# Splitting the first modulation into two column parts, and turning the order of two MLP steps, in a hybrid attention block

## The reference

```
c_act = silu(c)
mod   = c_act @ w_ada + b_ada            # 1024 -> 6 * 1024
sh1, sc1, gt1, sh2, sc2, gt2 = split(mod, 6)
h = rmsnorm(x, g_norm1) * (1 + sc1) + sh1
proj = h @ w_in          # queries, keys, values of three attention branches, indexer, gates
...                      # indexer scores -> top 128 keys, three attentions, gated merge
x = x + gt1 * (merged @ w_out)
h2 = rmsnorm(x, g_norm2) * (1 + sc2) + sh2
f_g, f_u = split(h2 @ w_gate_up, 2)
x = x + gt2 * ((silu(f_g) * f_u) @ w_down)
out = rmsnorm(x, g_final)
```

## Time and profile before

| | us |
|---|---|
| median of 3 runs | 1027.21 (1025.36 to 1028.98) |
| profiled execution, its time | 1024.62 |
| profiled execution, its span | 1022.8 |
| PE busy | 979.8 (96%) |
| DVE, ACT, POOL busy | 487.1, 382.2, 90.5 |
| first pass of the first projection starts at | 43.97 |
| tile 6 starts at | 80.42 |

### The profile page before, as it was taken

One profiled execution on the slowest core, in us unless ns is written; L12 is line 12 of the kernel. 1 busy time (PEld: TensorE's weight loads), 2 busy tenths in 40 slices (PEclk: granted clock), 3 DMA queues, 4 the chain that ended last, 5 costly groups with the idle time before them and its releaser, 6 DMA issues.

```text
span 1022.8 us, 12488 instructions
## 1 busy us (share of the span) xinstructions
PE 979.8 (96%) x4831; PEld 798.5 (78%) x4831; DVE 487.1 (48%) x826; ACT 382.2 (37%) x677; POOL 90.5 (9%) x130
## 2 busy tenths in 40 slices
PE   2699999999999999999999999999999999999997
PEld 0677988878877777778888888988888888888875
DVE  4845688743335435654647374733343343331323
ACT  4434522345555656642222223432232322221312
POOL 3000000000035432200000002000000000000401
PEclk9799999999999999999999999999999999999999
DMA  8693234321221201164555662123334434232312
GB/s 308 236 294 109 71 99 131 119 83 42 91 99 41 62 22 42 32 205 131 185 193 172 211 225 88 63 83 103 103 109 157 144 104 144 83 103 83 124 41 83
DMA packets 86082, 123.11 MB, mean 120 GB/s; under 512 B 4792, under 2 KB 67861, under 8 KB 85906
## 3 DMA queue, kind: packets, MB, share of 16 engines
q1 hardware_dynamic: 85506, 116.25, 34.8%
q0 software_dynamic: 528, 6.22, 2.1%
HBM read 119.77 MB, written 8.45 MB: 125 GB/s over the span
## 4 chain that ended last, share of the span: by engine, by line
PE 89%; DMA 4%; DVE 3%; ACT 2%; SPq 2%; issue 1%; POOLq 0%; POOL 0%; ACTq 0%; DVEq 0%
PE tile_ps L804 19%; PE tile_ps L806 18%; PE tile_ps L805 18%; DMA w_raw<-in_w_in_dram 4%; PE t_ps L968 2%; PE s_ps L950 2%; PE o_ps L997 2%; SPq L547 1%; PE o_ps L1146 1%; PE o_ps L1144 1%; PE t_ps L1145 1%; PE s_ps L1145 1%; PE s_ps L1144 1%; PE t_ps L1144 1%; PE o_ps L1145 1%; PE s_ps L1146 1%
## 5 line engine op out<-in xcount | busy, mean ns | idle before, releaser
L804 PE MATMUL tile_ps<-h_hi,w_hi 128*128 128x512 f32 x784 | 312.9, 399 | 6.5 <-DVE h_lo L1641 4.2
L806 PE MATMUL tile_ps<-h_hi,w_lo 128*128 128x512 f32 x784 | 306.8, 391 | 0.0
L805 PE MATMUL tile_ps<-h_lo,w_hi 128*128 128x512 f32 x784 | 306.5, 391 | 0.0
L1601 DVE TENSOR_TENSOR w_lo<-w_raw,w_hi 128x2048 fp32r<-128x2048 f32 (+2 forms) x62 | 135.8, 2190 | 165.4 <-ACT w_hi L1251 165.2
L804 PEld LDWEIGHTS tile_ps<-h_hi,w_hi 128*128 128x128 f32 x784 | 147.5, 188 | 46.4 <-issue 13.1
L806 PEld LDWEIGHTS tile_ps<-h_hi,w_lo 128*128 128x128 f32 x784 | 147.3, 188 | 31.9
L805 PEld LDWEIGHTS tile_ps<-h_lo,w_hi 128*128 128x128 f32 x784 | 147.6, 188 | 29.4 <-issue 0.2
L1251 ACT ACTIVATE w_hi<-w_raw 128x2048 fp32r<-128x2048 f32 (+2 forms) x62 | 111.4, 1797 | 38.3 <-DMA w_raw<-in_w_in_dram 11.7
L1598 DVE TENSOR_TENSOR t_lo<-t_raw,t_hi 128x2048 fp32r<-128x2048 f32 (+1 forms) x15 | 32.8, 2184 | 85.8 <-ACT t_hi L1249 85.8
L1376 ACT ACTIVATE nl<-nl,cst 128x256 f32<-128x256 f32 (+3 forms) x81 | 43.1, 532 | 50.0 <-DVE cst L1772 49.9
L1249 ACT ACTIVATE t_hi<-t_raw 128x2048 fp32r<-128x2048 f32 (+1 forms) x15 | 27.0, 1799 | 81.7 <-PE s_ps L1146 53.5
(11 more groups left out here) (338 smaller groups left out, 1575.0 us busy)
## 6 DMA issues: line engine op xcount, KB each, us to landing
w_raw<-in_w_in_dram SPq DMA_DIRECT2D x31, 1024.0 KB, 5.3
w_raw<-in_w_gate_up_dram SPq DMA_DIRECT2D x22, 1024.0 KB, 7.3
ada<-in_w_ada_dram SPq DMA_DIRECT2D x24, 512.0 KB, 13.5
ada<-in_w_ada_dram SPq DMA_DIRECT2D x12, 1024.0 KB, 5.4
...
```

Of the source, the lines that this page charges most:

```text
L804: pe.matmul(tile_ps[b][0:mw, :], wh, x_hi[:, kx, :], start=start, stop=False)
L805: pe.matmul(tile_ps[b][0:mw, :], wh, x_lo[:, kx, :], start=False, stop=False)
L806: mm = pe.matmul(tile_ps[b][0:mw, :], wl, x_hi[:, kx, :], start=False, stop=stop)
L1601: dve.tensor_tensor(w_lo[s][:, 0:kt, :], w_raw[s][:, 0:kt, :], w_hi[s][:, 0:kt, :].bitcast(F32), ALU.subtract) \
```

## The change

The modulation's columns are taken in two parts, for k-tiles 0 to 4 (640 columns of shift and of scale together) and 5 to 7 (384 columns each). In part 0 the first two k-tiles of `w_ada` are not summed by DVE but multiplied on PE directly; the sums over partitions are written as 100 equal columns each. The products with `keep_busy` write a bank that nobody reads. POOL makes the modulated k-tiles (`hidden_full`), ACT rounds straight out of `x_T`, DVE subtracts. The first five k-tiles of the query tiles are multiplied before part 1 of the modulation is known, and part 1's partition sums stand inside the fourth tile. The query tiles take four banks, the key tiles two others. x comes in four DMAs with chunk 0 right behind, the five small broadcasts behind the power. In the MLP ACT rounds chunk 2 ahead of the first silu, at the end `down` of chunk 10 is done for two blocks ahead of chunk 11, and the last half block is stored from ACT's queue.

```diff
+FIRST_KTS = (range(0, 5), range(5, 8))
+SUM_W = 100
+N_DIRECT = (2, 0)
 # SP
-            for b in range(2):
-                sp.dma_start(x_nat[:, 2 * b:2 * b + 2, :], ...).then_inc(x_in[b], 16)
-            for g in range(2):
+            for b in range(NBLK):
+                sp.dma_start(x_nat[:, b, :], a["x"][0, b * P:(b + 1) * P]).then_inc(x_in[b], 16)
+            load(0, [(KT, 0, cols(COL_IQ, CW))])
+            for q, kts in enumerate(FIRST_KTS):
                 for k in range(KT):
-                    sp.dma_start(ada1[g][k][:], a["w_ada"][0][k * P:(k + 1) * P, g * D:(g + 1) * D]) ...
-            load(0, [(KT, 0, cols(COL_IQ, CW))])
-            load(1, [(KT, 0, cols(COL_IQ + CW, CW))])
+                    sp.dma_start(ada1[q][k][:], w_ada[k * P:(k + 1) * P, 0:2, kts[0] * P:(kts[-1] + 1) * P]) ...
+                if q == 0:
+                    load(1, [(KT, 0, cols(COL_IQ + CW, CW))])
...
-                for half_ in range(2):
+                for half_ in ((0, 1) if b < NBLK - 1 else (1,)):
 # POOL: lamv and gkv DMAs stand behind power(1, rs_x, ms_x, 4); then
+            def hidden_full(kt):
+                pool.wait_ge(amp_ready, 1 if kt in FIRST_KTS[0] else 2)
+                pool.wait_ge(xt_read, kt + 1)
+                if kt >= 4:
+                    pool.wait_ge(h_ready, kt - 3)
+                pool.tensor_scalar(h_full[kt % 4][:], x_T[:, kt, :], amp1[:, kt:kt + 1], shift1[:, kt:kt + 1],
+                                   ALU.mult, ALU.add).then_inc(h_full_made, 1)
 # PE
+            def direct(k):
+                pe.wait_ge(ada1_in[0][k], 16)
+                for g in range(2):
+                    for m in range(5):
+                        pe.matmul(sum_ps[g][:, m, :], ada1[0][k][:, g, m * P:(m + 1) * P],
+                                  c_act[:, k:k + 1].to_broadcast([P, SUM_W]), start=k == 0 and m == 0, stop=False)
+            def keep_busy(n):
+                for _ in range(n):
+                    pe.matmul(tile_ps[1][:], ones[:], x_T[:, 0, :], start=True, stop=True)
+            direct(0)
             pe.wait_ge(x_scaled, NBLK)
...
+            def mod_part(q):
+                n = len(FIRST_KTS[q])
+                pe.wait_ge(ada1_added, [KT - 2, 2 * KT - 2][q])
+                for g in range(2):
+                    for m in range(n):
+                        mm = pe.matmul(sum_ps[g][:, m, :], ada1_sum[q][:, g, m * P:(m + 1) * P], ones[:, 0:SUM_W], ...)
+                mm.then_inc(mod1_made, 1)
+            for kt in range(KT):
+                turn_x(kt)
+            pe.wait_ge(xt_read, 1)
+            keep_busy(1)
+            direct(1)
+            keep_busy(1)
+            mod_part(0)
+            keep_busy(2)
+            chunk_ready(0)
+            for kt in FIRST_KTS[0]:
+                for t in range(2):
+                    query_part(t, (kt,))
+            chunk_ready(1)
+            query_part(2, FIRST_KTS[0])
+            query_part(3, range(0, 2))
+            mod_part(1)
+            query_part(3, range(2, 5))
+            for kt in FIRST_KTS[1]:
+                for t in range(2):
+                    query_part(t, (kt,))
+            for t in range(2, 4):
+                query_part(t, FIRST_KTS[1])
+            s = chunk_ready(2)
+            project(s, 4, h_hi, h_lo, straight, 0, bank=key_ps[0])
+            project(s, 5, h_hi, h_lo, straight, P, 72, bank=key_ps[1])
...
             chunk_ready(CH_DN + 10)
+            down(10, 0)
+            down(10, 1)
+            chunk_ready(CH_DN + 11)
             for b in range(NBLK):
-                down(10, b)
-                if b == 0:
-                    chunk_ready(CH_DN + 11)
+                if b >= 2:
+                    down(10, b)
                 down(11, b).then_inc(dn_made, 1)
 # ACT: scales x blocks 0 and 1 only; make_hi(0); 8 copies to x_T; then
+            for kt in FIRST_KTS[0]:
+                hidden_hi(kt)
+                if kt == 2:
+                    make_hi(1, None)
...
+            gate_up(early=True)      # make_hi(CH_GU + 2) ahead of the two silu
+            act.wait_ge(o_done[0], NBLK)
+            act.dma_start(out[0, S - P:S, 0:HW], o_nat[:, NBLK - 1, 0:HW]).then_inc(stored, 16)
 # DVE: scales x blocks 2 and 3; then
             make_lo(0)
+            add_part(0, range(2, KT))     # 6 instructions of 1280 columns
+            amplitude(0)
+            hidden_lo(0, 1)
+            hidden_lo(1, 2)
+            add_part(1, range(0, 1))      # 8 of 768 columns in all
+            hidden_lo(2, 3)
+            add_part(1, range(1, 2))
+            hidden_lo(3, 4)
+            add_part(1, range(2, 3))
+            hidden_lo(4, 5)
             make_lo(1)
+            add_part(1, range(3, KT))
+            amplitude(1)
+            for kt in FIRST_KTS[1]:
+                hidden_lo(kt, kt + 1)
```

More of the change, by code:

```diff
@@ L383, in hybrid_block @@
         mod_made = sem("mod_made")
+        mod1_made = sem("mod1_made")
         consts = sem("consts")
@@ L794, in tile_start, with project @@
                 return b
-            def project(s, t, x_hi, x_lo, kts, m0, mw=P, i=0, per=0, first=True, last=True, ready=None):
-                b = tile_start(t, i, per) if first else use(t, i, per)[0]
+            def project(s, t, x_hi, x_lo, kts, m0, mw=P, i=0, per=0, first=True, last=True, ready=None, bank=None):
+                b = tile_start(t, i, per) if first and bank is None else use(t, i, per)[0]
+                dst = tile_ps[b] if bank is None else bank
                 for n, (kw, kx) in enumerate(kts):
@@ L1270, in _ @@
                                accum_out=ms_x[:, b:b + 1]).then_inc(x_sq, 1)
-            act.wait_ge(pow_out, 1)
-            for b in range(NBLK):
-                act.activation(x_nat[:, b, :], x_nat[:, b, :], ACT.Copy, scale=rs_x[:, b:b + 1]).then_inc(x_scaled, 1)
             for j, ps in enumerate((t_ps[0], t_ps[1], s_ps[1])):
@@ L1628, in _ @@
[L1628 to L1642 removed]
+            dve.sem_inc(cols_ready, 1)
@@ new lines, in _, with add_part @@
+            dve.wait_ge(x_sq, NBLK)
+            dve.tensor_scalar(ms_x, ms_x, EPS, None, ALU.add).then_inc(pow_in, 1)
+            dve.wait_ge(pow_out, 1)
+            for b in range(2, NBLK):
+                dve.tensor_scalar(x_nat[:, b, :], x_nat[:, b, :], rs_x[:, b:b + 1], None, ALU.mult) \
+                    .then_inc(x_scaled, 1)
+            def add_part(q, ks):
+                for k in ks:
+                    dve.wait_ge(ada1_in[q][k], 16)
+                    total = ada1_sum[q][:]
+                    if k == N_DIRECT[q]:
+                        ins = dve.tensor_scalar(total, ada1[q][k][:], c_act[:, k:k + 1], None, ALU.mult)
+                    else:
+                        dve.wait_ge(ada1_added, k - N_DIRECT[q] + (KT - 2) * q)
+                        ins = dve.scalar_tensor_tensor(out=total, in0=ada1[q][k][:], scalar=c_act[:, k:k + 1],
+                                                       in1=total, op0=ALU.mult, op1=ALU.add)
+                    ins.then_inc(ada1_added, 1)
@@ new lines, in amplitude @@
+            def amplitude(q):
+                dve.wait_ge(mod1_made, q + 1)
+                k0, n = FIRST_KTS[q][0], len(FIRST_KTS[q])
+                for g in range(2):
+                    c0 = 8 * g + k0
+                    ins = dve.tensor_tensor(mod[:, c0:c0 + n], sum_ps[g][:, 0:n, 0], b_ada[:, c0:c0 + n], ALU.add)
+                link(ins)
+                dve.scalar_tensor_tensor(out=amp1[:, k0:k0 + n], in0=scale1[:, k0:k0 + n], scalar=1.0,
+                                         in1=g_n1[:, k0:k0 + n], op0=ALU.add, op1=ALU.mult).then_inc(amp_ready, 1)
```

159 lines of the change are left out of this document (81 added, 78 removed).

## The result

The changed kernel took 1017.45 us (median of 4 runs, 1015.18 to 1017.59), the kernel before on the same chip 1027.38 (4 runs, 1025.36 to 1028.98): a ratio of 0.9905, 95% interval 0.9888 to 0.9923. Forecast were 1016.5 and a range of 1012.5 to 1022.0; the time lies in it, 0.95 us above the value. The profiled execution took 1017.55 with a span of 1015.4, so 7.4 less of span than the profile of before had. The medians differ by 9.9. Both the size of the terms and that gap of 2.5 are what the rest of this document is about. One later execution of the kernel before (beside e9) took 1243.53 us at a mean granted clock of 0.753 and is left out everywhere.

The account below looks back on a forecast made before the run. PE's own work was taken as 89% of the span, so gains come from its waits, mostly in the first 80 us. 7.0 + 1.2 + 2.1 + 0.4 = 10.7 off 1027.2 gave 1016.5 us, range 1012.5 to 1022.

Parts of the forecast that it names:

- x at 11.2: Start: with the small broadcasts behind the power, x is there at 11.2 instead of 13.6, a gain of 2.4 us.
- Sum of part 0: Start: DVE's adds of part 0 end at 30.7, with the data there at about 29, just ahead of the last add.
- I take the clock as held: Start: PE idles 2.7 us before `mod_part(0)`, the full clock stays, and its 20 instructions take 2.3 us.
- The rival: Start: clock lost before `mod_part(0)`, which costs 2.2 more, some 12 passes 0.2 each; 4.6 us in all, 1021; chance 0.18.
- Blocking of POOL and DVE: First k-tiles: POOL and DVE instructions exclude each other; PE waits 0.9 for k-tile 2 and 1.1 for chunk 1.
- Tile 6 at 73.4: Projection: tile 6 could start at 73.4 instead of 80.4.
- after 77: Projection: the forecast is wrong if tile 6 starts after 77.
- 7.0: Start: gain in us up to tile 6, bounds 3 and 9.4.
- Chunk 4: Projection: loaded from 62.4 beside the bias rows, there at about 80, wanted at 86.7, so not late.
- MLP 1.2: MLP: rounding the chunk ahead of the silu removes PE's wait of 1.12 and 0.1 more, a gain of 1.2 us.
- `w_down` 2.1: Last chunks: a second block of chunk 10 covers PE's wait of 1.96, plus 0.1; 2.1 us gained.
- Last store 0.4: End: ACT issues one of SP's two last DMAs beside it, a gain of 0.4 us, bounds -0.4 and 0.4.

Follow-up runs that it names:

- e9: The kernel before, unchanged, run again for a second profile: 1026.59 us (one execution).
- e8: The changed kernel with the five small broadcasts back in front of the power of x: 1016.21 us, ratio .9907 to the kernel before.
- e6: The changed kernel with partition sums 8 columns wide instead of 100: 1016.67 us, ratio .9909 to the kernel before.
- e3: The changed kernel with the modulated k-tiles (`h_full`) made by ACT instead of POOL: 1018.63 us, ratio .9921 to the kernel before.
- e2: The changed kernel with the five small broadcasts moved behind the fifth `h_full`: 1013.13 us, ratio .9868 to the kernel before.

## Why the prediction was right, and where its steps were not

The time was right to 1 us, the start was not, and that the two errors nearly cancel is luck. The steps, by their own words:

- **x at 11.2**: right to the hundredth (11.20), and the cause too. But the 2.4 us were no gain here. The broadcasts, moved behind the power, fell into the load of `w_ada`, which then ended as late as with the broadcasts in front (30.08 against 30.38 in e8).
- **Sum of part 0, "done at 30.7"**: 31.8. The adds themselves were right (6.52 / 4 = 1.63, forecast 1.69), and the data were indeed "just ahead of the last add", but at 30.08 and not at "about 29", and the load was hardly ahead of the three adds before it: the load set when they began, and from there both ran in step. The forecast had counted the broadcasts in: 6.3 MB behind x at 0.41 MB/us end at 26.6, so some 2.4 of its 29 are theirs, and they cost 2.8. It asked only for the last k-tile, and only whether it was late.
- **"I take the clock as held"**: this failed. PE's gap was 3.14 and not 2.7, and `mod_part(0)` took 4.10, not 2.3. The limit of 3.3, read from the one fall in the trace of before, was none: in e9 the clock fell 1.0 after work had ended, and in e6 with a gap of 1.49. The rival had it at 0.18 and 4.6 us, "`mod_part(0)` costs 2.2 more and some 12 passes 0.2 each"; the first half came true (1.8), the second did not, the passes were 0.23 apart, and in e6, where six of them were cold, they cost nothing.
- **Blocking of POOL and DVE**: right in kind. The single steps stretched more than forecast (POOL 1.37 each, DVE's add 1.45 for 1.06), and the waits that PE had of it were smaller: 0.25 and 0.32 for k-tiles and 0.5 for chunk 1, forecast 0.9 and 1.1. The working has a slip: its five subtractions, three adds and three POOL steps add up to 8.2, not to the 7.4 from 34.9 to 42.3; measured from the first subtraction to the split of chunk 1 are 7.3, so the number was right and its terms were not. e3 shows the cause: with POOL silent the same add takes 1.01. The Trainium skill, page "SBUF — State Buffer", section "Who interferes with whom", has the two engines exclude each other for such instructions; the traces agree, with these numbers.
- **Tile 6 at 73.4**: 76.69 and 76.53, so by the forecast's own line ("after 77") close to wrong. 7.0 was 3.7 to 4.3. With the broadcasts out of the way (e2) the same steps end at 72.06. The terms of the difference of 3.3 are 1.1 for the late sum, 1.8 for the clock, 0.2 less between the products and the first pass, and 0.6 more from there to tile 6. Of these 0.6, k-tile 5 is 0.3 late against its forecast distance from the first pass (56.76), tile 4 another 0.2 (65.53, where PE waits 0.31 for chunk 2), and the rest is in its 48 passes.
- **Chunk 4**: rounding began when its load was there at 83.5, split done at 87.8, wanted at 89.9: no wait, 2 us of slack.
- **MLP 1.2**: right; `f_t` waits no more, and pass by pass the difference of the two kernels grows there by 1.4.
- **`w_down` 2.1**: the wait went, and the difference grows by 2.2 between the first profiles. In e9, and by the mean clocks in about half of the executions of before, the wait also cost the clock: 3.8 in all. This is the term that makes up for the start.
- **Last store 0.4**: 0, inside its bounds.

So the sum was 10.7 = 7.0 + 1.2 + 2.1 + 0.4, and against the second profile of before it came out (1024.8 - 1015.3 = 9.5) as 4.3 (80.86 - 76.53) + 1.4 + 3.8 + 0, all to 0.1. Against the first profile it was 7.4 = 3.7 + 1.4 + 2.2 + 0, again to 0.1. The total was right by two errors of opposite sign: a start over-sized by about 3 and a `w_down` under-sized by 1.7 wherever before lost its clock. That loss could not be read from the one profile of before, which had the lucky case. What could be seen is that the start's sum had no slack: the last k-tile was reckoned just ahead of its add, and PE's gap 0.6 under the one fall that the trace had. Both went the wrong way together, since a late k-tile makes a late sum and with it a longer gap.
